# Loading and turning the prompt's first block inside the sample's front, and waiting later for the front's stores

## The reference

```python
def decoder_layer(h, mem_k, mem_v, conv_prev, ssm_prev, k_buf, v_buf, ...):
    xn = rmsnorm(h, g_mix)
    z, xbc, dt_raw, q, k, v = jnp.split(xn @ w_in, SPLITS, axis=-1)
    y_ssd, new_conv, new_ssm = ssd_branch(z, xbc, dt_raw, ...)   # Mamba-2 scan, 8 heads x 64
    y_att, new_k, new_v = swa_banded(...) or swa_with_buffer(...)  # window 128, 8 heads
    h = h + jnp.concatenate([y_ssd, y_att], axis=-1) @ w_out
    h = h + cross_attention(rmsnorm(h, g_cross), mem_k, mem_v, w_cq, w_co)
    hn = rmsnorm(h, g_ffn)
    h = h + (jax.nn.silu(hn @ w_gate) * (hn @ w_up)) @ w_down
    return h, new_conv, new_ssm, new_k, new_v
```

## Time and profile before

| | |
|---|---|
| median of three runs | 2998.0 us (2993.47 to 3001.1) |
| profiled execution, its own time | 3001.78 us |
| its span | 2999.9 us |
| mean granted TensorE clock | 0.969 |
| TensorE, share busy | 95% |
| VectorE, ScalarE, GpSimd, share busy | 48%, 39%, 33% |
| DMA, mean | 101 GB/s |

### The profile page before, as it was taken

The page is one execution under the profiler, slowest core; times in us unless marked ns, Lnnn a source line. Parts: engine busy times, 40 slices in busy tenths (PEclk is TensorE's granted clock), DMA queues, the critical chain, the costliest instruction groups (busy, mean ns, idle before and its releaser), DMA issues. The chain is left out here.

```text
span 2999.9 us, 34694 instructions
## 1 busy us (share of the span) xinstructions
PE 2836.5 (95%) x13537; PEld 2269.7 (76%) x13537; DVE 1451.5 (48%) x2190; ACT 1167.1 (39%) x1875; POOL 1002.4 (33%) x451
## 2 busy tenths in 40 slices
PE   7858978999999999999999999999999997999998
PEld 3436866788877877878778878878778776888886
DVE  3244556455665246556663265556652435222224
ACT  2224554444354234543453244443452234322222
POOL 1112203333333433333234433333334431333331
PEclk9879998999999999999999999999999998999998
DMA  9352365322222335232223354222223341222221
GB/s 309 114 148 64 113 189 145 97 85 81 71 70 86 97 102 174 76 85 81 71 71 98 97 163 106 84 82 66 72 83 99 106 152 36 85 78 83 79 84 58
DMA packets 415093, 303.03 MB, mean 101 GB/s; under 512 B 48075, under 2 KB 384079, under 8 KB 413890
## 3 DMA queue, kind: packets, MB, share of 16 engines
q1 hardware_dynamic: 412474, 294.41, 32.8%
q10 hardware_dynamic: 1880, 6.34, 0.6%
q0 software_dynamic: 576, 0.07, 0.0%
HBM read 277.90 MB, written 23.85 MB: 101 GB/s over the span
## 5 line engine op out<-in xcount | busy, mean ns | idle before, releaser
L1539 POOL TENSOR_TENSOR w_lo<-w_raw,w_hi 128x1024 fp32r<-128x1024 f32 x400 | 974.3, 2439 | 1795.0 <-ACT w_hi L1553 1795.0
L1553 ACT ACTIVATE w_hi<-w_raw 128x1024 fp32r<-128x1024 f32 x400 | 421.9, 1056 | 551.6 <-PE G L2846 270.4
L2532 PE MATMUL L<-xa_h,w_hi 128*128 128x512 f32 x1184 | 474.5, 401 | 0.0
L2533 PE MATMUL L<-xa_h,w_lo 128*128 128x512 f32 x1184 | 463.7, 392 | 0.0
L2534 PE MATMUL L<-xa_l,w_hi 128*128 128x512 f32 x1184 | 463.4, 391 | 0.0
L2532 PEld LDWEIGHTS L<-xa_h,w_hi 128*128 128x128 f32 x1184 | 223.8, 189 | 54.0 <-issue 6.7
L2534 PEld LDWEIGHTS L<-xa_l,w_hi 128*128 128x128 f32 x1184 | 223.6, 189 | 48.1
L2533 PEld LDWEIGHTS L<-xa_h,w_lo 128*128 128x128 f32 x1184 | 223.9, 189 | 45.8 <-issue 1.0
L2532 PE MATMUL L<-xb_h,w_hi 128*128 128x512 f32 x576 | 232.4, 404 | 8.7 <-DVE xb_l L1964 8.7
L2533 PE MATMUL L<-xb_h,w_lo 128*128 128x512 f32 x576 | 226.2, 393 | 0.0
L2534 PE MATMUL L<-xb_l,w_hi 128*128 128x512 f32 x576 | 225.7, 392 | 0.0
(11 more groups left out here) (560 smaller groups left out, 5003.1 us busy)
## 6 DMA issues: line engine op xcount, KB each, us to landing
w_raw<-in_w_down_dram SPq DMA_DIRECT2D x88, 512.0 KB, 3.4
w_raw<-in_w_gate_dram SPq DMA_DIRECT2D x66, 512.0 KB, 3.8
w_raw<-in_w_up_dram SPq DMA_DIRECT2D x66, 512.0 KB, 3.8
w_raw<-in_w_in_dram SPq DMA_DIRECT2D x56, 512.0 KB, 3.8
xt<-xT_dram SPq DMA_DIRECT2D x56, 256.0 KB, 4.2
w_raw<-in_w_gate_dram SPq DMA_DIRECT2D x44, 256.0 KB, 2.8
w_raw<-in_w_up_dram SPq DMA_DIRECT2D x44, 256.0 KB, 3.1
fwin<-in_w_in_dram SPq DMA_DIRECT2D x8, 1156.0 KB, 10.7
```

Of the source, the lines that this page charges most:

```text
L1539: pool.tensor_tensor(w_lo[:, n % RING, 0:w], w_raw[:, n % RING, 0:w], w_hi[:, n % RING, 0:w].bitcast(F32), ALU.subtract)\
L1553: act.activation(w_hi[:, n % RING, 0:w], w_raw[:, n % RING, 0:w], ACT.Copy)\
L2532: pe.matmul(acc, wh, rh, start=(k == 0), stop=False)
L2533: pe.matmul(acc, wl, rh, start=False, stop=False)
```

## The change

The work on the first four chunks of x moves from the start of the prompt's block into the front, in between its last steps, and so do the loads of the first three panels and the split of the first two. The front no longer waits for its stores: they count on semaphores that outlive the block (`early`), and the prompt's block waits for them where it first overwrites what they read. To fit, `xin0` lies where the front's `w_cq` lay, and the square's scrap output where memory keys lay.

```diff
@@ SP, end of the front
-                for bb in range(NB):
-                    sp.wait_ge(f["so_sb"], bb + 1)
-                    sp.dma_start(s_ssm[0, bb]..., stN[:, bb]).then_inc(f["out"], 16)
-                sp.wait_ge(f["x_sb"], 3)
-                sp.dma_start(hs_dram.ap(), fxin[:]).then_inc(f["out"], 16)
-                sp.dma_start(xs_dram.ap(), x3[:]...).then_inc(f["out"], 16)
-                sp.wait_ge(f["out"], 16 * (2 + 2 + NB + 2))
+                sp.wait_ge(f["wq"], 1)
+                for c in range(C):
+                    sp.dma_start(xin0[:, c, :], x_prompt[0, c * P:c * P + P, :]).then_inc(f[f"x0_in{c}"], 16)
+                sp.wait_ge(f["mkt"], 16)
+                for n in range(RING):
+                    for dst, src in panel_dmas(w_raw[:, n, :], panels[n][0]):
+                        sp.dma_start(dst, src).then_inc(early[f"w_in{n}"], 16)
+                def state_out(bb):
+                    sp.wait_ge(f["so_sb"], bb + 1)
+                    sp.dma_start(s_ssm[0, bb]..., stN[:, bb]).then_inc(early["late_out"], 16)
+                for bb in range(4):
+                    state_out(bb)
+                sp.wait_ge(f["h"], 2)
+                sp.dma_start(hs_dram.ap(), fxin[:]).then_inc(early["hs_out"], 16)
+                sp.wait_ge(f["x_sb"], 3)
+                sp.dma_start(xs_dram.ap(), x3[:]...).then_inc(early["hs_out"], 16)
+                for bb in range(4, NB):
+                    state_out(bb)
@@ GpSimd, end of the front
+                for n in range(AHEAD):
+                    pool.wait_ge(early["hi_ready"], n + 1)
+                    pool.tensor_tensor(w_lo[:, n, :], w_raw[:, n, :], w_hi[:, n, :].bitcast(F32), ALU.subtract)\
+                        .then_inc(early["lo_ready"], 1)
@@ ScalarE: squares of chunks 0, 1 before the score's exp, of 2, 3 behind it; panels behind oD
+                for c in range(2, C):
+                    act.wait_ge(f[f"x0_in{c}"], 16)
+                    act.activation(xjunk[:], xin0[:, c, :], ACT.Square, accum_out=ssx[:, c:c + 1]).then_inc(f["x0_sq"], 1)
+                    act.drain()
                 state_back(0, 4)
...
                 act.activation(oD[:, 0, :], G[:, 3, :], ACT.Copy).then_inc(f["od"], 1)
+                for n in range(AHEAD):
+                    act.wait_ge(early[f"w_in{n}"], 16 * len(panels[n][0]))
+                    act.activation(w_hi[:, n, :], w_raw[:, n, :], ACT.Copy).then_inc(early["hi_ready"], 1)
@@ VectorE, behind sX
+                for c in range(C):
+                    dve.wait_ge(f["x0_t"], c + 1)
+                    dve.tensor_copy(xT0[:, :, c * P:c * P + P],
+                                    G[:, 1:3, :].rearrange("p a (i t) -> p (a i) t", t=P)).then_inc(f["x0_ev"], 1)
...
                 dve.wait_ge(f["cpv"], 2)
                 dve.tensor_copy(oD[:, 1, :], G[:, 4, :]).then_inc(f["od"], 1)
+                dve.wait_ge(f["x0_rb"], 1)
+                dve.tensor_copy(RB, G[:, 5, :])
@@ TensorE
-                state_back(0, 4)
+                for c in range(C):
+                    pe.wait_ge(f[f"x0_in{c}"], 16)
+                    if c >= 1:
+                        pe.wait_ge(f["x0_ev"], c)
+                    if c == 2:
+                        state_back(0, 2)
+                    for i in range(KT):
+                        last = pe.transpose(G[:, 1 + i // 4, ...], xin0[:, c, i * P:i * P + P], ident[:])
+                    last.then_inc(f["x0_t"], 1)
+                state_back(2, 4)
...
+                pe.wait_ge(f["x0_diag"], 1)
+                pe.matmul(G[:, 5, :], ones[:], diag[:], start=True, stop=True).then_inc(f["x0_rb"], 1)
+                pe.wait_ge(f["x0_ev"], C)
                 pe.wait_ge(f["od"], 2)
@@ SP, the prompt's block
-                for n in range(NPAN):
+                for n in range(RING, NPAN):
                     if n == RING:
+                        sp.wait_ge(s["hs_out"], 32)
+                        sp.wait_ge(s["late_out"], LATE_OUT)
                         sp.dma_start(mem[:], ...).then_inc(s["mem_in"], 16)
@@ VectorE, the prompt's block; ScalarE waits for late_out ahead of the first q
-                for c in range(C):
-                    x_chunk_dve(dve, c)
-                r_group(dve, 0, 1)
-                diagonal(rx[:, 1, 0:C])
-                row_back(0, -1)
+                dve.wait_ge(s["hs_out"], 32)
```

More of the change, by code:

```diff
@@ L458, in build @@
         flip = held("flip", [P, P])
+        rx = held("rx", [P, 3, 16])
+        ssx = rx[:, 0, :]
         xsl = at("xsl", O_ZS, [P, KT, S])
@@ L555, in build @@
         oS = rest("oS", [P, CH, S])
-        assert free_at[0] <= arena_bytes
+        assert free_at[0] <= keep[0] - 192
+        early = {n: whole.enter_context(nc.semaphore("e_" + n))
+                 for n in [f"w_in{r}" for r in range(RING)] + ["hi_ready", "lo_ready", "late_out", "hs_out"]}
+        LATE_OUT = 16 * (2 + 2 + NB)
         front = Phase(["made", "mask", "consts", "pv_in", "par_in", "params", "pvt", "pv_sb", "rowt", "rsb", "rows_out",
-                       "cn_in", "snk_in", "x_in", "sc_in", "sw_in", "st_in", "mk_in", "mv_in", "wo_in", "wq_in", "wc_in", "out"]
+                       "cn_in", "snk_in", "x_in", "sc_in", "sw_in", "st_in", "mk_in", "mv_in", "wo_in", "wq_in", "wc_in",
+                       "x0_in0", "x0_in1", "x0_in2", "x0_in3", "x0_sq", "x0_t", "x0_ev", "x0_diag", "x0_rb"]
                       + [f"win_in{k}" for k in range(KT)]
@@ L1171, in _ @@
                 new_state(2, 4)
-                state_back(0, 4)
+                for c in range(C):
+                    pe.wait_ge(f[f"x0_in{c}"], 16)
[4 more added lines that the diff above has]
+                    for i in range(KT):
+                        last = pe.transpose(G[:, 1 + i // 4, (i % 4) * P:(i % 4) * P + P], xin0[:, c, i * P:i * P + P], ident[:])
+                    last.then_inc(f["x0_t"], 1)
+                state_back(2, 4)
                 pe.wait_ge(f["cpn"], 1)
@@ L1530, in _ @@
                                    pattern=[[1, P]], channel_multiplier=1).then_inc(s["consts"], 1)
-                for n in range(NPAN):
+                for n in range(AHEAD, NPAN):
                     if n == 13:
@@ L1827, in last_ffn @@
                                .then_inc(s["S_ycp"], 1)
-                for c in range(C):
-                    x_chunk_act(act, c)
-                for n in range(AHEAD):
-                    round_panel(n)
                 for i in range(KT):
@@ L2867, in turn_y @@
                     last.then_inc(s["y_t"], 1)
-                for c in range(C):
-                    x_chunk_pe(pe, c)
-                norm_rows(0, -1)
                 pe.wait_ge(s["consts"], 1)
```

93 lines of the change are left out of this document (43 added, 50 removed).

## The result

The changed kernel takes 2982.9 us (median of 5 runs, 2980.9 to 2983.7), the kernel before 3000.0 us in the same comparison: a ratio of 0.9944, 95% interval 0.9929 to 0.9958. That is 17 us less.

The account below looks back on a forecast made before the run. TensorE, 95% busy, bounds the kernel, so only its standstill around the change of blocks can be won. 26.0 removed - 12.6 longer front - 1.0 block start = 12.4 us; 2998.0 - 12.4 = 2985.6 us, range 2978 to 2994.

Parts of the forecast that it names:

- the likeliest case: The forecast itself, given 67%: gains of 7.2 to 17.2 us, or 2981 to 2991 us.
- the range of gains: Gains from the bounds of the costs: 7.2 to 17.2 us, around the forecast 12.4.
- Removed, 26.0 us: Change of blocks: 21.6 us between block start and norm1_t, plus 4.3 us after the last state store, go away.
- The longer front, 12.6 us: Front's last chain: turns and copies of x plus the spreading matmul add 8.8 to 16.4 us, middle 12.6.
- my bounds of 7.8 and 12.5: Front, until the turns of sX end: 7.8 us later at the high clock, 12.5 at the low one.
- the spreading matmul: Front, ahead of the turns of oD: adds 1.0 us at the high clock, 2.1 at the low one.
- the low-clock case: Front with TensorE at 1.2 GHz: 16.4 us longer, including 1.8 for a slower product with memV.
- The start of the new block, 1.0 us: Prompt's block: norm1_t beside GpSimd's memsets and a late first instruction cost 0 to 2.4 us, taken as 1.0.
- Nothing late behind it: Prompt's block: transfers after its start, toep with at least 6 us of cover, and the next panel arrive in time.
- TensorE's low clock: Rival, 12%: low clock through the rest of the front, cost 26.2 us, gain gone, 2999 us; half gives 2994.
- The slow start: Rival, 9%: the new block's start costs up to 6.1 us in place of 1.0, giving 2990.7 us.
- The slower case, late transfers: Rival, 4%: toep or the panel behind it lands over 36 us after block start, gain lost; at 45 us, 3007.

Follow-up runs that it names:

- experiment a: Kernel before, with only the front's stores counted on semaphores that outlive the block and waited for in the prompt's block; 2995.1 us, ratio 0.9982.
- Experiment b: Changed kernel with the waits for all stores put back at the end of SP's queue in the front; 2982.7 us, ratio 0.9943.
- experiment d: Changed kernel with chunks 0 and 1 in two bank pairs, chunks 2 and 3 turned in the last norm's gap, all squares before the exp; 2972.3 us.
- experiment c: Changed kernel with the three panels' loads and two splits back in the prompt's block, x still in the front; 2992.0 us, ratio 0.9972.
- experiment g: Changed kernel with extra turns into an unused PSUM bank to keep TensorE busy; 2978.9 us in one execution.
- experiment f: Changed kernel with 2.9 MB more copies queued between the slabs and toep in the prompt's block; 2987.1 us in one execution.

## Why the prediction was right, step by step

The time, 2982.9, lies 2.7 us under the forecast of 2985.6 and inside the likeliest case's own range. The gain is further off than the time: 12.4 us were forecast, the medians show 17.1, the upper edge of the range of gains, and the trace 15.7 at the first projection (16.6 from the states' add). The time came closer because the kernel before measured 3000.0 in the comparison and not the 2998.0 that I had subtracted from, and that is luck. The 3.3 us by which 15.7 exceeds 12.4 are mis-sized terms, taken one by one below; rounded, they are 2.1 in the front, 1.0 at the new block's start and 0.3 in the barrier.

- **Removed, 26.0 us: right.** `norm1_t` follows the block's start at once (21.6 us), and experiment a gives 3.9 us for the stores where I had 4.3. Experiment b adds that the wait is about 2 us of it and, by difference, the order of the stores the rest.
- **The longer front, 12.6 us: mis-sized by 2.1.** The last store is issued by 190.85 in place of 180.37, 10.5 us. Of these, 0.85 is a later start (145.15 against 144.30). It is none of the moved work: at the first break in the input projection the two traces are already 1.4 us apart (33.57 against 32.17), and in experiment d, with the same loads moved, the start is at 144.25. Without it the front is 9.6 us longer, and the term is 3.0 too large and not 2.1. All of the 9.6 lies between the first turns and `memV` (16.15 against 6.56), within my bounds of 7.8 and 12.5 and near their middle. The term that failed is the spreading matmul: I put 1.0 to 2.1 us for it on the path, and it cost 0.1. It runs at 164.91 while TensorE would have waited for VectorE's copy of `oD` at 165.06 anyway, 0.82 us of idle time that stood in the earlier trace rows ahead of 155.37. A row's idle time says what fits in ahead of it; I read it for ScalarE and not here. Also, the clock was back before the product with `memV` (3.68 us), so what I had counted for a slow one, 1.8 us in the low-clock case and half of it in the middle, didn't come.
- **The start of the new block, 1.0 us: it cost nothing.** From the block's start to the first projection 2.29 us passed, exactly as from `norm1_t` before. The memsets did not hold VectorE (1.42 us for the first two `norm1_t`, as in the earlier trace rows). The contention that the Trainium skill states in "GPSIMD Engine Reference" for operations with two SBUF inputs is real in this case, as the 2.63 us of experiment c show, but there against a GpSimd operation on two inputs. Here it was GpSimd's last small operation that took 0.50 us, where before it took 0.29 with VectorE idle. It takes 0.49 or 0.50 in all seven kernels in which `norm1_t` starts with the block, and 0.29 in the two others:

```profile
189.08 0.29 POOL L1529 TENSOR_SCALAR_AFFINE_SELECT flip<-flip 128x128 f32<-128x128 f32 x1
```

Of the branch's price (the Trainium skill, "Runtime: NRT & Kernel Launch", Instruction fetch mechanics) nothing is to be seen after the block's start. SP's 2.4 us of waiting for TensorE's sequencer stand in the barrier of every kernel here; whether a fetch is in them no run shows, nor that each engine takes two such branches.
- **Nothing late behind it: right for TensorE, wrong in a detail.** I wrote that ScalarE would wait for no panel, and it waits 4.53 us. That wait reached TensorE nowhere: it turns the bias at 216.10 without having been idle. `toep` had a cover of about 6 us (issued at 201.43, landed 8.5 us later), the bound that I gave. One reading of the stretches was too broad: the change of blocks isn't the only place where TensorE stands still (in the kernel before it is busy for 77.3 of the 100 us from 361.86 on), but it is the one that this change touches.
- **The sum as measured.** 26.0 + 0.3 (a barrier of 3.0 for 3.3) - 10.5 = 15.8 us, against 15.7 in the trace. The other 2.3 us of the profiled execution's 18.0 came later. Between the first blocks the distance of the two traces wanders. The largest step is in the same 400 us of the program, first the kernel before, then the changed one (TensorE busy, granted clock, DMA share, GB/s):

```profile
811.86:1211.86 400.00, 392.26 (x1841) 0.98 0.36 106
```

```profile
796.14:1196.14 400.00, 390.62 (x1859) 1.00 0.35 106
```

The kernel before ran part of it at the low clock, the other didn't. The distance between experiment a and the kernel before, read at GpSimd's subtractions, moves too: from 4.8 us at the first ones to -0.6 and up to 7.4, to end at 4.5, though nothing behind the first projection is changed there. So I take this for the scatter of single executions and for nothing that the change does; why the clock falls in one execution and not in another there, I didn't find out.

The rivals: TensorE's low clock did come (experiment g: 2.5 us) but ended before the long products, where it would have been dear. The slow start didn't come. The slower case, late transfers, didn't come: `toep` landed about 16 us after the block's start where 36 would have used up the gain, and in experiment f 2.9 MB more made TensorE wait 3.2 us.

## What to carry to other kernels

A change of phase is worth taking apart even at 1% of the run: move the next phase's first steps into the idle time of each engine ahead of it, and order the stores so that the one issued last isn't the one waited for. What is moved must fit the gaps where it lands, which the idle time beside each row of the trace shows: the same 32 turns and four copies cost 9.6 us as a ladder through one pair of PSUM banks (2.5 of them by the low clock), 2.4 us (9.0 against 6.6) with two pairs, and nothing when half of them stood where TensorE and ScalarE wait for the norm. And compare two traces from a mark that the change can't move: here the front alone arrived up to 2.3 us apart.

## What was not expected of the hardware

- Two VectorE-GpSimd collisions behave differently: a `norm1_lo` (two SBUF inputs) beside GpSimd's subtraction of 128x1024 took 2.63 us instead of 0.68 and ended 0.5 us behind that subtraction, while two `norm1_t` beside GpSimd's memsets took 1.42 us, as without them, and it was GpSimd's small select that took 0.50 instead of 0.29 us.
- The last of four state stores (256 KB each, issued within 3.1 us) was waited for 2.0 us; the last of two scratch stores of the same size, issued within 1.2 us right behind a state store, 3.1 us.
- In the changed front TensorE's granted clock fell to 1.2 GHz after 3.6 us in which the engine was idle, stayed there through a group of eight turns (1.88 us) and a pause of 1.36 us, and was back at 2.4 GHz near 157, right behind 3.6 us of turns without a pause (153.08 to 156.72). In the kernel before it fell after 2.0 us of idle time and was back near 150.5, behind 2.8 us of turns without a pause (147.38 to 150.18). In both, turns were the only work that TensorE did before the clock came back, and in experiment g extra turns kept it at 2.4 GHz.
